# A two-layer transformer step on one core: in the second attention, five output tiles begun before the last head, and the squares' sums and rotations placed further behind the projections

## What is computed

```python
def gqa_axial_mixer(u, uc, w_in, q_norm, k_norm, w_out):
    # project(): q, k, v = split(t @ w_in); q = rmsnorm(q, q_norm); k = rmsnorm(k, k_norm)
    q, k, v = project(u)          # 256 latent tokens
    qc, kc, vc = project(uc)      # 256 context tokens
    q, k = apply_rope(q, cos, sin), apply_rope(k, cos, sin)
    k_all, v_all = concatenate([kc, k]), concatenate([vc, v])
    return softmax(q @ k_all.T * 128 ** -0.5) @ v_all @ w_out
```

## Time and profile before

| What | Value |
|---|---|
| median of three runs | 2390.12 us |
| profiled execution, its own time | 2389.94 us |
| its span, first to last instruction | 2388.1 us |
| mean granted clock of TensorE | 0.997 of full speed |
| TensorE busy with matmuls | 2315.0 us, 97% |
| VectorE, ScalarE, GpSimd busy | 1306.9, 974.7, 1338.8 us |
| the attention of the second layer | about 1450 to 1571 us of the span |

### The profile page before, as it was taken

How to read it: one execution, slowest core, us unless ns; L and a number is a source line. 1 busy time by engine, 2 the same in 40 slices (tenths; PEclk the granted TensorE clock), 3 DMA queues, 4 the chain that set the end, 5 groups by cost and what they waited for, 6 DMA issues and landing times.

```text
span 2388.1 us, 36102 instructions
## 1 busy us (share of the span) xinstructions
PE 2315.0 (97%) x14528; PEld 2069.3 (87%) x14528; DVE 1306.9 (55%) x2196; ACT 974.7 (41%) x1605; POOL 1338.8 (56%) x700
## 2 busy tenths in 40 slices
PE   7999999999889999999999999899999999999998
PEld 5888889777688888899888897799999999999998
DVE  8898296666678982967332036564324315533331
ACT  4322224455442322244223235455445444555443
POOL 4564465222135654654444443178878887468886
PEclk9999999999999999999999999999999999999999
DMA  6555362211025553624553331145545564345554
GB/s 271 212 190 180 110 219 85 71 62 54 28 79 212 194 177 110 219 94 178 194 176 110 97 102 62 45 158 185 179 149 196 176 188 163 106 152 184 183 178 134
DMA packets 97509, 350.09 MB, mean 147 GB/s; under 512 B 10945, under 2 KB 10945, under 8 KB 96961
## 3 DMA queue, kind: packets, MB, share of 16 engines
q1 hardware_dynamic: 97344, 347.81, 43.2%
HBM read 346.71 MB, written 1.05 MB: 146 GB/s over the span
## 4 chain that ended last, share of the span: by engine, by line
PE 60%; DVE 5%; ACT 2%; issue 2%; DMA 1%; POOL 1%; SPq 0%; DVEq 0%; ACTq 0%
PE psum L1589 19%; PE psum L1593 19%; PE psum L1590 19%; POOL w_lo L776 1%; ACT w_hi L796 1%; PE psum L1938 1%; DMA w_raw<-in_ffn_out 0%; DVE stat L1505 0%; DVE psum L1141 0%; DVE psum L1221 0%; DVE h L1227 0%; PE psum L1910 0%; DVE pcomb L1414 0%; DVE u_lo L1445 0%; ACT prob L1055 0%
## 5 line engine op out<-in xcount | busy, mean ns | idle before, releaser
L776 POOL TENSOR_TENSOR w_lo<-w_raw,w_hi 128x1024 fp32r<-128x1024 f32 (+3 forms) x696 | 1338.6, 1945 | 1032.3 <-ACT w_hi L796 1031.7
L1589 PE MATMUL psum<-u_hi,w_hi 128*128 128x256 f32 (+2 forms) x2912 | 973.9, 334 | 12.1 <-POOL w_lo L776 8.2
L1593 PE MATMUL psum<-u_lo,w_hi 128*128 128x256 f32 (+2 forms) x2912 | 948.7, 326 | 3.3 <-DVE u_lo L1213 2.0
L1590 PE MATMUL psum<-u_hi,w_lo 128*128 128x256 f32 (+2 forms) x2912 | 947.4, 325 | 0.0
L796 ACT ACTIVATE w_hi<-w_raw 128x1024 fp32r<-128x1024 f32 (+1 forms) x522 | 537.3, 1032 | 439.9 <-PE psum L1593 345.1
L1589 PEld LDWEIGHTS psum<-u_hi,w_hi 128*128 128x128 f32 x2912 | 555.2, 191 | 75.3 <-issue 24.4
L1593 PEld LDWEIGHTS psum<-u_lo,w_hi 128*128 128x128 f32 x2912 | 554.6, 190 | 51.8 <-DVE u_lo L1213 3.8
L1590 PEld LDWEIGHTS psum<-u_hi,w_lo 128*128 128x128 f32 x2912 | 555.5, 191 | 45.3 <-issue 3.4
L1589 PE MATMUL psum<-gu_hi,w_hi 128*128 128x256 f32 (+1 forms) x1188 | 379.3, 319 | 1.0 <-POOL w_lo L776 1.0
L1590 PE MATMUL psum<-gu_hi,w_lo 128*128 128x256 f32 (+1 forms) x1188 | 378.2, 318 | 0.0
L1593 PE MATMUL psum<-gu_lo,w_hi 128*128 128x256 f32 (+1 forms) x1188 | 378.1, 318 | 0.0
(11 more groups left out here) (180 smaller groups left out, 1989.2 us busy)
## 6 DMA issues: line engine op xcount, KB each, us to landing
w_raw<-in_ffn_in SPq DMA_DIRECT2D x264, 512.0 KB, 3.5
w_raw<-in_ffn_out SPq DMA_DIRECT2D x96, 448.0 KB, 3.4
ada_hi<-in_ada_w SPq DMA_DIRECT2D x48, 512.0 KB, 5.2
ada_lo<-in_ada_w SPq DMA_DIRECT2D x48, 512.0 KB, 5.2
w_raw<-in_ffn_out SPq DMA_DIRECT2D x48, 512.0 KB, 3.6
ada_out<-in_ada_w SPq DMA_DIRECT2D x32, 512.0 KB, 3.8
w_raw<-in_b_qkv SPq DMA_DIRECT2D x30, 512.0 KB, 3.4
w_raw<-in_da_in SPq DMA_DIRECT2D x24, 512.0 KB, 3.5
```

The source lines that it names most:

```text
L776: last = pool.tensor_tensor(w_lo[:, slot, w], w_raw[:, slot, w], w_hi[:, slot, w].bitcast(F32), ALU.subtract)
L1589: mm(out, w_hi[:, slot, w], x_hi, start=start and n == 0, stop=False)
L1590: mm(out, w_lo[:, slot, w], x_hi, start=False, stop=False)
L1593: last = mm(out, w_hi[:, slot, w], x_lo, start=False, stop=stop and n == len(ks) - 1)
```

## The change

The second attention begins five output tiles instead of two ahead of its last head. Output tiles 0 to 3 get the blocks of seven heads early, tile 4 those of four heads. The pieces of tiles 2 and 3 lie in the other half of the banks 0 and 1 (numbers 8 and 9 in the code), so tiles 0 and 1 are read out only when tiles 2 and 3 are done too. The early pieces use a head one unit later than before. The squares' sum of a head is due two pieces behind its projection instead of one, its rotation three pieces behind the sum instead of two. `LEAD`, `QUOTA` and `FILLS` of this attention are set anew. ScalarE prepares the weights of output tiles 4 and 5 while the last head is worked. The number of matmuls is the same.

```diff
+LEFT = 8
+EARLY = {"da": (7, 7), "ga": (7, 7, 7, 7, 4)}
...
-LEAD = {"da": 4, "ga": 9}
-QUOTA = {"da": [3, 3, 3, 3] + [3, 3, 2] * 8, "ga": [2, 2, 3, 3, 3] + [2] * 7}
-FILLS = {"da": [0] * 28 + [1, 1, 2, 2, 1, 1], "ga": [0] * 12 + [2, 2, 1, 1, 1, 1], "b2": [0] * 21 + [3, 3, 3, 3, 3]}
+LEAD = {"da": 4, "ga": 12}
+QUOTA = {"da": [3, 3, 3, 3] + [3, 3, 2] * 8, "ga": [2] * 12}
+FILLS = {"da": [0] * 28 + [1, 1, 2, 2, 1, 1], "ga": [0] * 12 + [3, 3, 2, 2, 2, 4], "b2": [0] * 21 + [3, 3, 3, 3, 3]}
...
-                pending.append(("ss" if it["norm"] else "rot" if it["rope"] else "vtr", it, clock + (1 if it["norm"] else 2)))
+                pending.append(("ss" if it["norm"] else "rot" if it["rope"] else "vtr", it, clock + 2))
...
-            pending.append(("rot", it, clock + 2))
+            pending.append(("rot", it, clock + 3))
...
-        last = sets[-1]["s"]
-        filler = [(d, k, min(k + 2, last), min(k + 2, last)) for k in range(0, last, 2) for d in range(2)]
+        last, tiles = sets[-1]["s"], len(EARLY[kind])
+        filler = [(d, k, min(k + 2, EARLY[kind][d]), min(k + 2, last)) for k in range(0, last, 2) for d in range(tiles)
+                  if k < EARLY[kind][d]]
+        filler.sort(key=lambda x: x[0] >= 4)
...
-        done = heads
+        done, heads_before = (heads, heads) if kind == "da" else (heads_before, heads)
...
+        shares = 2 if b["kind"] == "ga" and j < 2 else 0
+        return tile_used, b["t_out"] + parts * (j + 1 + shares)
...
+            if bank >= LEFT:
+                act.wait_ge(y_evac, b["pc"] + i - 1)
...
-                    if kind == "da" and u["set"]["s"] == DA_HEADS - 1:
+                    if kind != "b2" and u["set"]["s"] == DA_HEADS - 1:
                         heads_to(min(b["t_out"] + 4 + u["U"] - u["set"]["first_unit"], b["t_out"] + RING - 1))
...
-                early = b["kind"] in ("da", "ga") and j < 2
+                begun = EARLY.get(b["kind"], ())[j:j + 1]
```

More of the change, by code:

```diff
@@ L119, in out_pieces @@
     if tok == LAT:
-        return [(j, LAT, {"ffn": 4 + j % 2, "b2": j % 2, "ga": (0, 1, 4, 5)[j % 4]}[kind]) for j in range(CH)]
+        return [(j, LAT, {"ffn": 4 + j % 2, "b2": j % 2, "ga": (0, 1, 0 + LEFT, 1 + LEFT, 4, 5, 4, 5)[j]}[kind]) for j in range(CH)]
     if kind == "ffn":
@@ L303, in mixer_plan @@
     LAG = 2
+    heads_before = 0
     for U in range(len(units) + LAG):
-        done = heads
+        done, heads_before = (heads, heads) if kind == "da" else (heads_before, heads)
         u = units[U] if U < len(units) else None
@@ L597, in full_chunks, with piece_bank @@
         return range(2 * (idx - 3), 2 * (idx - 2)) if 3 <= idx < 7 else ()
+    def piece_bank(bank, tok):
+        return psum[:, bank, tok] if bank < LEFT else psum[:, bank - LEFT, 0:SEQ]
     def bank_before(b, i):
@@ L609, in piece_end @@
         parts = len(out_parts(b["kind"]))
-        return tile_used, b["t_out"] + parts * (j + 1)
+        shares = 2 if b["kind"] == "ga" and j < 2 else 0
+        return tile_used, b["t_out"] + parts * (j + 1 + shares)
     LATE = {"ffn": {"m": 0, "v3": 1}, "da": {"r1": 0, "r4": 1, "m": 2, "v0": 3, "v2": 4, "v4": 5}}
@@ L889, in piece_square @@
             act.wait_ge(*piece_end(b, i))
+            if bank >= LEFT:
+                act.wait_ge(y_evac, b["pc"] + i - 1)
             if b["ac"] + i >= 2:
                 act.wait_ge(yacc_ready, summed(b, i - 2))
-            scalar.activation(sq[:, i % 2, tok], psum[:, bank, tok], ACT.Square).then_inc(ysq_ready, 1)
+            scalar.activation(sq[:, i % 2, tok], piece_bank(bank, tok), ACT.Square).then_inc(ysq_ready, 1)
         def transition(b, nb):
@@ L1239, in piece @@
                 gate = g_col[:, 3 * m + b["part"], j:j + 1]
-                last = vec.tensor_scalar(y[:, j, part], psum[:, bank, part], gate, None, ALU.mult)
+                last = vec.tensor_scalar(y[:, j, part], piece_bank(bank, part), gate, None, ALU.mult)
             last.then_inc(y_evac, 1)
@@ L1801, in output @@
                     ends = p == len(parts) - 1
-                    if early:
-                        last = blocks(t % RING, psum[:, bank, tok], moving(tok), [CH - 1], first=CH - 1, start=False,
-                                      ready=ctx_ready if tok == FULL else ready)
+                    if begun:
+                        last = blocks(t % RING, piece_bank(bank, tok), moving(tok), range(begun[0], CH), first=begun[0], start=False,
+                                      stop=b["kind"] != "ga" or j >= 2, ready=ctx_ready if tok == FULL else ready)
                     else:
@@ L1955, in mixer @@
                         bank = next(bank for j, _, bank in b["pieces"] if j == d)
-                        blocks(t % RING if k0 else split(t), psum[:, bank, tok],
-                               lambda k: (o_hi[:, k, tok], o_lo[:, k, tok]), range(k0, k1), first=k0, start=k0 == 0, stop=False)
+                        if bank == 4:
+                            pe.wait_ge(S["exp_done"], exps_through(kind, 2 * GA_HEADS - 1))
+                        blocks(t % RING if k0 else split(t), piece_bank(bank, tok),
+                               lambda k: (o_hi[:, k, tok], o_lo[:, k, tok]), range(k0, k1), first=k0,
+                               start=k0 == 0 and bank < LEFT, stop=False)
                 elif op == "oss":
```

## The result

| | before | after |
|---|---|---|
| median of five runs | 2389.14 us | 2410.88 us |
| lowest and highest | 2388.42, 2393.72 | 2409.2, 2412.51 |
| profiled execution, span | 2388.1 us | 2409.5 us |
| granted clock, mean | 0.997 | 0.991 |

The ratio is 1.0088, with a 95% interval of 1.0077 to 1.0099: the change costs 0.88%. Forecast were 2409.5 us and +0.81%.

The account below looks back on a forecast made before the run. TensorE, busy 97% of the span, was taken as the bound. On 2389.94 us, 11.1 + 1.0 + 1.6 - 0.5 = +13.2 gave 2403.1; clock falls of 6.5 made 2409.6, rounded to 2409.5; range 2401 to 2413.

Parts of the forecast that it names:

- The chain: Odd unit's scores to next even unit's, through maximum, exponential, `o_hi`, `pcomb`, rotation: 8.10 us, four times; +11.1 us in all.
- the longer first one: First odd-to-even stretch, from unit 5: VectorE comes late to the maximum; +1.0 us, between 0 and 1.74.
- The held `pcomb`: `pcomb` takes 1.74 us beside GpSimd's `w_lo`, 0.40 without; 1.34 us in each of four odd-to-even stretches.
- The clock: TensorE falls to half clock behind four score waits and one output-stage wait, 1.3 us each: +6.5 us.
- A: Whole kernel: TensorE waits and its clock falls behind the waits; 2409.5 us, own range 2405 to 2413, chance 0.60.
- B: Whole kernel: TensorE waits but its clock holds, since busy stretches break the waits; 2403.1 us, chance 0.27.
- The fifth fall: Output stage: one fall of TensorE's clock for 4.8 us of waits there, costing 1.3 us.
- The early pieces: Before the last values: 36 matmuls, 4.3 us, and a squares' sum, 0.4, move in, filling 3.1 idle; net +1.6 us.
- The output stage: After the last values: fewer matmuls, but waits for tile 6's weights and a `y`; 19.0 to 18.5 us, -0.5.
- the first part: Output-stage wait for `w_lo` of tile 6: ready at 9.6 us after the last values, TensorE there at 7.9.
- the list of signs: What the later profile would show if right, including output-stage waits for `w_lo` and a `y`, about 4.6 us together.
- The head of the stage: Before unit 5's scores: `LEAD` 12 and first quotas move projection pieces ahead; 0 us, within 0.5 either way.

Follow-up runs that it names:

- the steps: Changed kernel with GpSimd making this attention's `w_lo` in four steps of 256 columns instead of one of 1024: 2407.14 us, ratio 1.0061.

## Why the prediction was right

**The chain.** Forecast 8.10 us from odd to even and 1.0 more on the first; measured 8.13 and 9.24, and 8.13 again with the due counts alone. The reason given for the longer first one, a late maximum, is in the trace. Putting the rotation back took the waits away. With three falls in it, units 5 to 12 were forecast 16.0 us longer and came out 16.2 longer.

**The held `pcomb`.** Forecast 1.34 us for each chain; with GpSimd kept away each was 1.31 shorter. The rule of the Trainium skill ("SBUF — State Buffer", section "Who interferes with whom") that the one who starts first has the port for the whole instruction fits the three forms: 1.80, 0.86 and 0.49 us. My reading of it for the steps was wrong, in the experiment and not in the prediction: I counted the shorter hold of `pcomb`, and not that the next step would hold the instruction behind it.

**The clock.** A (waits and a fallen clock) held, B fell: all four waits were followed by a stretch at 0.50, each worth 1.36 us where 1.3 was forecast; adding work in the waits showed the price. The trace agrees here with "HAM oscillation — how this bites in real kernels" in "TensorE: Matmul & The Clock Gate" of the Trainium skill, turn after turn; with GpSimd kept away that holds in two turns of four. What decides behind which wait the clock falls stays open. The fifth fall was mis-sized: in the output stage it lasted 6.8 us. 114 matmuls at 0.12 and the wait of 4.9 are 18.6 us, and the stage took 21.2, so it cost 2.6, twice the term. Why some falls last 6.8 us and not 3.4 the runs do not explain.

**The early pieces.** Forecast +1.6 and one fall from unit 12 to the last values, 2.9; measured +2.5, so +1.2 without the fall. Without the chain and at full clock it was +2.2 where the rest of the change stayed (the rotation sooner), and +0.6 with `LEAD`, `QUOTA` and the due counts of before. No run settles the term better than that.

**The output stage.** Forecast -0.5 and a fall of 1.3, +0.8; measured +1.9, for the longer fall. The wait was forecast at 4.8 in the sum (12.7 less 7.9; the list of signs has 4.6), in two parts, and came as one of 4.9, ended by the `y`; the first part is hidden in it. The mechanism is right step by step: `w_lo` at 9.9 us behind the last values and `y` at 13.1, forecast 9.6 and 12.7.

**The head of the stage.** Forecast 0 within 0.5; measured -0.5.

**Outside the stage.** Forecast 0; +4.8 ahead and -3.5 behind, between the two profiled executions. That these are falls of the clock in unchanged code is read from the traces and was not tested. The medians differ by 21.7 us, where 19.4 was forecast. That the stage's 20.1 came so close to the 19.7 is in part luck: the early pieces (-0.4) and the head (-0.5) nearly cancel the output stage (+1.1) and units 5 to 12 (+0.2).

**The range.** Its upper end, 2413, was said to hold falls of up to twice the length. Five such would add 6.5 us and the first chain 0.7, which is 2416.8; the range was narrower than its reason.

## What to carry to other kernels

Before an operation that feeds an in-order engine is moved later, follow its result through every engine's queue: here a rotation one place later stood behind work that needed the scores just issued, and turned a hidden step into a chain of 8 us. Work brought ahead of an idle stretch pays only if what remains behind still covers the ring of weights and the readout of the banks; take as much as that cover allows, not as much as fits. A long GpSimd instruction beside VectorE's critical one is better moved in time than cut in pieces, unless the work behind it is spread out, as in the output stage, where the pieces did help.

## What the runs showed of the hardware that was not expected

- Matmuls of ones in a wait, 2.84 us of them in each, made the program 4.7 us faster, and held the clock behind three waits of four.
- The length of the wait did not decide alone whether the clock fell: with GpSimd kept away it stayed at 1.00 behind a wait of 3.50 us and fell behind ones of 2.61 and 2.05.
- GpSimd's 1024 columns take 2.35 us in one instruction and 3.13 in four beside VectorE. Of `pcomb` and `rope_a`, the one that begins beside a step is stalled. Not every instruction of VectorE is: in the output stage after, a `y`, which reads PSUM, began beside a `w_lo` and took 0.47 us, where the sums, which read two tensors in SBUF, took over 2.

```profile
1585.06 0.47 DVE L1252 TENSOR_SCALAR y<-psum,g_col 128x256 f32<-128x256 f32 x1
```

- The stage starts between 1456.7 and 1463.9 us in the profiles of kernels whose code is the same up to there, but for the steps of the first `w_lo`. The latest two have 10.2 and 13.6 us at half clock between 600 and 760 us, the earliest none. So single times of this kernel tell less than the stage's length in the trace.
